# LayerNorm after two expert layers: from stages of their own into the last steps of the expert stages

## The reference, cut to what matters

```
x   = _layernorm(ALPHA * x   + g1 * y_lat, ln_w[layer, 0], ln_b[layer, 0])
f_lat = _peer(x * (1.0 + sc2) + sh2, ...)
x   = _layernorm(ALPHA * x   + g2 * f_lat, ln_w[layer, 1], ln_b[layer, 1])     # the norm of this case
ctx = _layernorm(ALPHA * ctx + cg2 * f_ctx, ln_w[layer, 1], ln_b[layer, 1])    # the same, first layer only
hl = x * (1.0 + sc1) + sh1                                                     # start of the next layer
hc = ctx * (1.0 + csc1) + csh1
```

## Time and profile before

| | before |
|---|---|
| median of 3 runs | 3768.81 us (3768.76 to 3774.37) |
| the profiled execution's own time | 3774.25 us |
| its span | 3772.4 us |
| PE busy | 3024.5 us (80%) |
| DVE busy | 1991.3 us (53%) |
| ACT busy | 791.2 us (21%) |
| POOL busy | 879.9 us (23%) |
| DMA | 1026.04 MB, 272 GB/s over the span |
| first norm stage with the barriers around it (end of last `take` to first `c_q` matmul) | 1845.9 to 1901.1 us |
| second norm stage with the barriers around it (end of last `take` to first `b_rms1` instruction) | 2945.4 to 2971.5 us |

### The profile page before, as it was taken

One profiled execution on the slowest core, in us unless ns is written; L12 is line 12 of the kernel. 1 busy time (PEld: TensorE's weight loads), 2 busy tenths in 40 slices (PEclk: granted clock), 3 DMA queues, 4 the chain that ended last, 5 costly groups with the idle time before them and its releaser, 6 DMA issues. The chain is left out here.

```text
span 3772.4 us, 28092 instructions
## 1 busy us (share of the span) xinstructions
PE 3024.5 (80%) x8564; PEld 1486.2 (39%) x8564; DVE 1991.3 (53%) x5057; ACT 791.2 (21%) x2002; POOL 879.9 (23%) x772
## 2 busy tenths in 40 slices
PE   7987788888888888777488667878877597897898
PEld 3444443333333333322243334333332355453663
DVE  1135567777777777776610756767776323223100
ACT  0112312222222222222101312222222130122000
POOL 0000014444444444444100003444444000000000
PEclk9996899999999999999788689999999898898999
DMA  5143229999999999999612247999999343323333
GB/s 195 57 157 112 90 114 427 427 427 427 427 427 423 423 421 417 426 416 427 262 45 91 90 157 322 427 427 427 427 427 427 142 139 116 112 105 130 112 134 122
DMA packets 238156, 1026.04 MB, mean 272 GB/s; under 512 B 41399, under 2 KB 46007, under 8 KB 137639
## 3 DMA queue, kind: packets, MB, share of 16 engines
q0 software_dynamic: 110592, 805.36, 50.8%
q1 hardware_dynamic: 126984, 217.63, 16.5%
q10 hardware_dynamic: 432, 1.31, 0.1%
HBM read 1023.10 MB, written 1.13 MB: 272 GB/s over the span
## 5 line engine op out<-in xcount | busy, mean ns | idle before, releaser
L1528 PE MATMUL l_peer_experts_acc<-l_peer_experts_ring,l_peer_experts_diag 128*128 128x512 f32 x1840 | 860.9, 610 | 217.3 <-ACT l_peer_experts_diag L1567 216.8
L1688 DVE SCALAR_TENSOR_TENSOR l_peer_experts_ring<-l_peer_experts_ring,h_tiles 128x1024 f32<-128x1024 f32 x460 | 563.6, 1225 | 287.4 <-DMA l_peer_experts_ring<-in_expert_rows,l_peer_experts_picks 283.9
L1528 PE MATMUL l_peer_experts_acc<-weight_slots,l_peer_experts_diag 128*128 128x512 f32 x1232 | 581.2, 614 | 150.9 <-ACT l_peer_experts_diag L1567 150.6
L1470 POOL DMA_INDIRECT weight_slots<-in_expert_rows,l_peer_experts_picks x308 | 348.1, 1130 | 1431.1 <-DVE l_peer_experts_picks L1647 1009.0
L1470 POOL DMA_INDIRECT l_peer_experts_ring<-in_expert_rows,l_peer_experts_picks x460 | 531.7, 1156 | 611.5 <-PE l_peer_experts_acc L1528 538.1
L1528 PEld LDWEIGHTS l_peer_experts_acc<-l_peer_experts_ring,l_peer_experts_diag 128*128 128x128 f32 x1840 | 337.4, 192 | 710.9 <-issue 397.3
L1688 DVE SCALAR_TENSOR_TENSOR weight_slots<-weight_slots,h_tiles 128x1024 f32<-128x1024 f32 x308 | 377.4, 1225 | 190.8 <-DMA weight_slots<-in_expert_rows,l_peer_experts_picks 188.3
L1528 PEld LDWEIGHTS l_peer_experts_acc<-weight_slots,l_peer_experts_diag 128*128 128x128 f32 x1232 | 227.9, 194 | 481.7 <-issue 274.7
L1560 ACT ACTIVATE l_peer_experts_gel<-l_peer_experts_dots 128x2 f32<-128x2 f32 x384 | 78.2, 204 | 1207.6 <-DVE l_peer_experts_ring L1688 727.1
L1567 ACT ACTIVATE l_peer_experts_diag<-const_ident,l_peer_experts_wgt 128x128 f32<-128x128 f32 x768 | 266.4, 394 | 225.8 <-DVE l_peer_experts_wgt L1664 209.8
L1495 PE MATMUL l_peer_experts_queries<-h_t,l_query_weights 128*128 128x512 f32 (+3 forms) x576 | 182.0, 461 | 3.9 <-PEq L61 3.9
(11 more groups left out here) (464 smaller groups left out, 3367.1 us busy)
## 6 DMA issues: line engine op xcount, KB each, us to landing
weight_slots<-in_w_mod SPq DMA_DIRECT2D x24, 2048.0 KB, 7.8
weight_slots<-in_w_in SPq DMA_DIRECT2D x20, 2048.0 KB, 7.7
l_query_weights<-query_weights SPq DMA_DIRECT2D x16, 1024.0 KB, 9.0
weight_slots<-in_w_mlp_up SPq DMA_DIRECT2D x8, 2048.0 KB, 7.8
weight_slots<-in_w_mlp_down SPq DMA_DIRECT2D x8, 2048.0 KB, 7.7
weight_slots<-in_gla_w_in SPq DMA_DIRECT2D x6, 2048.0 KB, 8.4
weight_slots<-in_ab_w_in SPq DMA_DIRECT2D x5, 2048.0 KB, 8.8
l_ln_rows<-mod_rows SPq DMA_DIRECT2D x16, 512.0 KB, 9.5
```

Source lines behind the costliest of these rows:

```text
L1470: pool.indirect_dma_start(rows(b, k, None), None, uv, bass.IndirectOffsetOnAxis(ap=picks[:, b % 4, k:k + 1], axis=0)).then_inc(landing(b, ...
L1528: ins = nc.tensor.matmul(acc[:, b % 2, c * BANK:(c + 1) * BANK], diag[:, k % DIAGS, :], row[:, c * BANK:(c + 1) * BANK], start=(k == 0), s ...
L1688: nc.vector.scalar_tensor_tensor(row, row, 1.0, h[:, tile_of(b), :], ALU.mult, ALU.mult, accum_out=dots[:, b % 2, k:k + 1]).then_inc(dotte ...
```

## The change

The two norm stages are gone. Their work is inside `stage_peer`:

- **Rows.** `LastNorm` puts gates, weight and bias (4 rows in the first layer, 3 in the second) into `wq_slots`. SP issues these loads in the expert stage as soon as the last projection is done.
- **Norm.** `normalise(tile, part)` splits the norm of one tile into seven parts on DVE. Each stands behind the dot of one k. In the first layer tile 0 has its parts in step 30, tile 1 in steps 30 and 31, tile 2 in step 31. In the second layer tile 0 has them in step 15. The last tile's seven parts come after the loop, behind the last `take`. The square roots stand in ACT's queue at fixed pairs of the last two steps (`root_at`), that of the last tile after the loop.
- **Modulation.** The four broadcast rows of scales and shifts and the two DVE instructions per tile are replaced. The scales and shifts are loaded as columns (`mod_cols`, four DMAs of 1024 single floats, first in SP's queue in the first layer's expert stage). PE transposes blocks of the normalised `x` instead of `h`, into the PSUM of the projections; ACT writes each block of 128x128 to `h_t` with the column of scales as its scale and that of shifts as its bias: eight instructions per tile instead of two. Tiles 0 and 1 are transposed ahead of k = 2 and k = 6 of the last step and modulated behind pairs 3 and 6; tiles 2 and 3 after the loop.
- **Weights.** SP issues `weights.begin` as soon as the last product has been added, with no row loads ahead of it.

```
 @block.sync
+    for i, (scale, shift) in enumerate(norm.mods):
+        for j, row in enumerate((scale, shift)):
+            sp.dma_start(mod_cols[:, i, j, :], row.rearrange("(c p) -> p c", p=P), allow_slow_non_contiguous=True).then_inc(mods_loaded, 16)
     ...
+    sp.wait_ge(q_done, len(units))
+    norm.load(sp, wq_slots, rows_loaded)
+    sp.wait_ge(added, steps * TOPK // 2)
+    weights.begin(sp)

+    norm_at, root_at = {}, {}
+    for tile in range(group - 1):
+        first, at, pair = {3: (steps - 2, (0, 1, 2, 3, 6, 7, 8), 1), 2: (steps - 2, (9, 10, 11, 12, 15, 16, 17), 6),
+                           1: (steps - 1, (5, 6, 7, 8, 11, 12, 13), 4)}[group - 1 - tile]
+        root_at[first, pair] = tile
+        for part, k in enumerate(at):
+            norm_at[first + k // TOPK, k % TOPK] = (tile, part)

 @block.tensor
+    def turn(tile):
+        pe.wait_ge(made, tile + 1)
+        if tile:
+            pe.wait_ge(emptied, 2 * tile)
+        else:
+            pe.wait_ge(q_taken, len(units))
+        for half in range(2):
+            for c in range(4):
+                at = (4 * half + c) * P
+                last = nc.tensor.transpose(q_ps[:, half, c * P:(c + 1) * P], x[:, tile, at:at + P], ident)
+            last.then_inc(turned, 1)
     ...
+        if norm.mods and b == steps - 1 and k in (2, 6):
+            turn(k // 4)
     ...
+    if norm.mods:
+        for tile in range(2, group):
+            turn(tile)

 @block.scalar
+    def modulate(tile):
+        i = norm.mod_of[tile]
+        for half in range(2):
+            act.wait_ge(turned, 2 * tile + half + 1)
+            for c in range(4):
+                k = 4 * half + c
+                last = nc.scalar.activation(h_t[:, k, tile * P:(tile + 1) * P], q_ps[:, half, c * P:(c + 1) * P], ACT.Identity,
+                                            scale=mod_cols[:, i, 0, k:k + 1], bias=mod_cols[:, i, 1, k:k + 1])
+            last.then_inc(emptied, 1)
     ...
+        if (b, j) in root_at:
+            root(root_at[b, j])
+        if norm.mods and b == steps - 1 and j in (3, 6):
+            if j == 3:
+                act.wait_ge(mods_loaded, 32 * len(norm.mods))
+            modulate(j // 3 - 1)
+    root(group - 1)
+    if norm.mods:
+        for tile in range(2, group):
+            modulate(tile)

 @block.vector
+    def normalise(tile, part):     # part 0: gate * y   1: ALPHA * x + y   2: bn_stats x2   3: bn_aggr, + epsilon
+        ...                        # part 4: wait for the root, reciprocal, (x - mean) * rstd   5: * weight   6: + bias
     ...
+        if (b, k) in norm_at:
+            normalise(*norm_at[b, k])
         if k % 2:
             weigh(b, k // 2)
     take(steps - 1)
+    for part in range(7):
+        normalise(group - 1, part)
```

More of the change, by code:

```diff
@@ L637, in load @@
             eng.dma_start(dst, src).then_inc(mod_sem if mod_sem is not None and i >= self.norm_rows else sem, 16)
[L640 to L737, removed]
@@ L1372, with __init__, row, load @@
 UV_SLOTS = 10
-def stage_peer(nc, name, h, h_t, group, n_groups, wq, wq_slots, wq_loaded, wq_before, k_t, uv, iota, ident, layer, y, slots, landed, before0):
+class LastNorm:
+    def __init__(self, gates, ln, mods=(), mod_of=()):
+        self.sources = [row for _, row in gates] + list(ln)
+        self.gate_of = {tile: i for i, (tiles, _) in enumerate(gates) for tile in tiles}
+        self.mods, self.mod_of = mods, mod_of
+        self.n_rows = len(self.sources)
+    def row(self, buffer, i):
+        return buffer.rearrange("p s k n -> p (s k n)")[:, i * D:(i + 1) * D]
+    def load(self, eng, buffer, sem):
+        for i, source in enumerate(self.sources):
+            eng.dma_start(self.row(buffer, i), source.partition_broadcast(P)).then_inc(sem, 16)
+    def gate(self, buffer, tile):
+        return self.row(buffer, self.gate_of[tile])
+    def weight(self, buffer):
+        return self.row(buffer, self.n_rows - 2)
+    def bias(self, buffer):
+        return self.row(buffer, self.n_rows - 1)
+def stage_peer(nc, name, h, h_t, group, n_groups, wq, wq_slots, wq_loaded, wq_before, k_t, uv, iota, ident, layer, y, slots, landed, before0, x, norm, weights):
     DIAGS = TOPK // 2
@@ L1434, in stage_peer @@
         share = scratch[:, 448:480].rearrange("p (i k) -> p i k", k=TOPK)
+        stats = st.sb("ln_stats", [P, 2, 6])
+        agg = st.sb("ln_agg", [P, group, 2])
+        std = st.sb("ln_std", [P, group])
+        rstd = st.sb("ln_rstd", [P, group])
+        mod_cols = st.sb("ln_mod_cols", [P, max(1, len(norm.mods)), 2, KC])
+        rows_loaded, mods_loaded, var_ready, std_ready, made, turned, emptied = (
+            st.sem(f"ln_{n}") for n in ("rows_loaded", "mods_loaded", "var_ready", "std_ready", "made", "turned", "emptied"))
         names = ("dotted added scored scores_read chosen gelu_done soft_in soft_out w_ready diag_ready sum_taken "
@@ L2513, in buffers, with peer @@
     return lambda name, shape, dt=F32: ctx.enter_context(nc.sbuf_tensor(name, shape, dt))
[L2516 removed]
+def peer(nc, weights, name, layer, group, n_groups, consts, a, wq, keys_t, h, h_t, y, landed, before0, x, norm):
     stage_peer(nc, f"{name}_experts", h, h_t, group, n_groups, *wq, keys_t[:, :, :], a["expert_rows"], consts["iota"][:, :], consts["ident"][:, :], layer, y,
[L2519 removed]
+               weights.slots[:, :, :, :], landed, before0, x, norm, weights)
 def mixer_ab(nc, weights, consts, a, cat, h_t, y, mod0, mod1):
@@ L2730, in build @@
                 peer(nc, weights, "l0_peer", 0, *L0_GROUP, consts, a, (wq, wq_slots[:, :, :, :], wq_loaded, 0), keys_t, h[:, :, :], h_t[:, :, :],
[L2731 to L2735, removed]
+                     y[:, :, :], landed, 0, x, LastNorm([((0, 1), row(0, True, 5)), ((2, 3), row(0, False, 5))], ln(0, 1),
+                                                        [(row(1, context, 1), row(1, context, 0)) for context in (True, False)], (0, 0, 1, 1)))
             mixer_c(nc, weights, consts, a, h, h_t, y, mod_args[1])
@@ L2747, in build @@
                 peer(nc, weights, "l1_peer", 1, LT, 1, consts, a, (wq, wq_slots[:, :, :, :], wq_loaded, 16 * HEADS * L0_GROUP[1] // 2), keys_t,
[L2748 to L2751, removed]
+                     h[:, 0:LT, :], h_t[:, :, :], y[:, 0:LT, :], landed, HEADS * TT * TOPK, x[:, 2:4, :], LastNorm([((0, 1), row(1, False, 5))], ln(1, 1)))
         second_block(nc, weights, consts, a, x[:, 2:4, :], x[:, 0:2, :], out)
```

29 lines of the change are left out of this document (added).

## The result

| | before | changed |
|---|---|---|
| median | 3771.59 us (3768.76 to 3774.49, 4 runs) | 3726.95 us (3718.44 to 3732.09, 4 runs) |
| ratio | | 0.9877, 95% interval 0.9866 to 0.9888 |
| span of the profiled execution | 3772.4 us | 3726.1 us |
| from first gather to last dot, first / second layer | 1292.1 / 651.4 us | 1298.2 / 655.3 us |
| from last dot to last sum, first / second layer | 6.24 / 6.24 us | 6.76 / 6.24 us |

The kernel is 1.2% faster: 44.6 us between the medians, 46.3 us between the two spans, 47.6 predicted.

What follows compares the result with a forecast made beforehand. DMA bytes bound the expert stages, and the tails between them are plain chains. Gains of 41.1 and 16.3 less 9.8 us for rows give 47.6, from 3768.81 to 3721.2 us; 3711 to 3735 for 8 in 10.

Steps and rivals of the forecast that it cites:

- Tail of the first layer: From the first layer's last sum to `c_q`: 14.1 us against 55.2, a gain of 41.1 us.
- Tail of the second layer: From the second layer's last sum to `b_rms1`: 9.8 us against 26.1, a gain of 16.3 us.
- The collision of the weights with `b_rms1`'s rows: Second layer's tail: early weight tiles may delay `b_rms1`'s row loads, up to 1.5 us possible, taken as 0.
- The rows: Seven 512 KB loads moved into the DMA-bound expert stages: 1.4 us each, 9.8 us lost, bounds 8.6 to 17.5.
- The columns: Four column loads at the start of the first expert stage, while the DMA is idle: cost 0.
- the slower rival: First expert stage: column loads share DMA engines with the gathers; at 20 us each the time is 3801 us; chance 0.02.
- The last steps: End of the expert loops: DVE, PE and ACT cover the parts, cost 0, bound 2 us a layer; falling behind, chance 0.12.
- the lag of 0.7 us: DVE in the last step: 0.7 us behind the pace at k = 13, gone at k = 14.
- PE: two turns of 2.0 us ... made up in two pairs, the second by k = 10: PE in the last step: two turns of 2.0 us beside 3.7 of 4.9 us per pair, made up, cost 0.
- the gap from the last landing to the last product: End of the last step: over 6.2 us here would show the prediction wrong.
- ScalarE's switches: ACT's roots in the loop: 2.8 us each without drain; draining rival 3725 to 3728 us, chance 0.09 together with dear rows.
- PE's clock: PE at `c_q` after the tail: no change in granted clock, with 2.6 us to either side.

Runs made afterwards that it cites:

- e2: The changed kernel with the seven broadcast rows loaded a second time behind the first, in the DMA-bound part; 3735.29 us.
- e4: The changed kernel with the second layer's three broadcast rows loaded at the start of its expert stage, into idle tiles of h and y; 3722.34 us, ratio 0.9872.
- e7: The changed kernel with sixteen instead of four column loads ahead of the query weights in SP's queue; 3724.35 us (1 run).
- e3: The changed kernel with tile 1 transposed ahead of k = 10 of the last step instead of k = 6; 3725.05 us.

## Why the prediction was right

The mechanism holds: tails that are a plain chain, a DMA-bound loop in which only the rows' bytes cost, and norm work that the loop covers. Term by term the sum is within 1.4 us: 40.7 gained for 41.1, 16.0 for 16.3, 9.9 lost for 9.8, and 0.5 lost at the last product for 0. That the profiled execution as a whole came within 1.2 us is in part luck: the stretches outside moved by 5.2 us down and 4.0 up and happened to cancel.

- **Tail of the first layer:** 14.1 us predicted, 1868.87 - 1854.35 = 14.5 measured. The eight ACTIVATEs took 2.9 us for 3.0, one of them 462 ns for 457. The missing 0.4 us is the end of the stage, 2.34 us from the last ACTIVATE to `c_q` for 1.8: I had 0.03 us per semaphore from one pair of stages, and the runs give 0.055 to 0.07.
- **Tail of the second layer:** 9.8 predicted, 10.1 measured, with 0.3 from the same cause. The collision of the weights with `b_rms1`'s rows didn't show: DVE waits 4.18 us for the rows, 4.90 before.
- **The rows:** 9.8 us predicted, 9.9 in the profile, 9.3 as the mean over the experiments (5.4 + 3.9). e2 shows the cost directly, and e4 that it goes where the DMA is idle. The 1.4 us a row was the least certain price; the 1.2 to 1.35 measured lie between it and the lower bound of 1.23. The last product came 8.5 us later than before: 6.0 by the rows, inside the "5 to 7", 1.9 by the later first gather and 0.5 by the stall below.
- **The columns** cost nothing that shows (e7); the slower rival falls with them. **The weights** for `c_q` were there in time: it started as soon as the barrier let it.
- **The last steps:** DVE waited for a landing again at k = 15 as predicted, but not at k = 14, where it ran straight on from k = 13. The dot of k = 13 starts at 1841.48, 4.88 us before the one of k = 15 that waits for its landing. That is two rows of the pace (4.92), so the lag of 0.7 us that I had counted isn't there. The step that failed is "PE: two turns of 2.0 us ... made up in two pairs, the second by k = 10". I had costed the turns as work and overlooked the wait in front of the second one: `emptied`, which ACT gives only after it has modulated tile 0, behind the diagonals of k = 6 and 7. It cost some 3 of the 4.1 us that PE stands there, and 0.5 us of the span (0.4 to 1.4 over the profiles), inside the 2 us a layer that I had as a bound, but for another reason. One sign that I had named for being wrong did appear: the gap from the last landing to the last product was to stay within 6.2 us and is 1853.09 - 1846.36 = 6.7. The kernel before has 6.20, so the sign left no room, and it caught this step. The turns themselves were too dear in my sum: 1.04 and 1.06 us for 2.0. ACT's covers were thinner than I had them: behind the three roots it still idled 0.5 to 0.9 us as predicted, but the gelu behind each modulation followed without a pause, where I had 0.7 us to spare.
- **ScalarE's switches:** no drain shows. Around the first root in the loop:

```profile
1779.01 0.69 ACT L1555 ACTIVATE l_peer_experts_diag<-const_ident,l_peer_experts_wgt 128x128 f32<-128x128 f32 x2 [0.52 <-DVE l_peer_experts_wgt L1662]
1779.72 1.28 ACT L1524 ACT_TABLE_LOAD   x1
1781.02 0.20 ACT L1524 ACTIVATE l_peer_experts_ln_std<-l_peer_experts_ln_agg 128x1 f32<-128x1 f32 x1
1781.24 1.28 ACT L1548 ACT_TABLE_LOAD   x1
1783.02 0.20 ACT L1548 ACTIVATE l_peer_experts_gel<-l_peer_experts_dots 128x2 f32<-128x2 f32 x1 [0.50 <-DVE l_peer_experts_ring L1716]
```

  Root and both loads take 2.8 us, and ACT then has 0.5 us to wait for its next dot. The Trainium skill's 2.66 us a switch ("ScalarE: Activation LUTs", section "What ACT_TABLE_LOAD costs") would have made this 5.5, an estimate; the measurement decides against it here.
- **PE's clock** before and after a tail: `c_q` took 15.45 us instead of 16.55, but 17.04 when the changed kernel was profiled again, and 15.5 to 17.1 in the experiments. So "no change" holds, and the 1.1 us aren't a gain of the change. The clock over the mixer, where the profiles differ by 10 us, was not in the prediction; only the 5.6 us between the runs before stood for it.

## What to carry to other kernels

Work moved from a stage of its own into a DMA-bound loop cost nothing here as long as its engine caught up before the last product, but each byte moved there with it cost its full share; so look for a time when the DMA is idle, and for idle memory, before placing a load. Cost a moved instruction with the waits in front of it, not only its duration: the one real stall came from a shared PSUM buffer whose release stood in another engine's queue. When a change is worth a few us in a long kernel, compare the stretches of the profiles that it touches, since the untouched ones alone scattered by more.

## What the runs showed of the hardware beyond that

- The end of a stage took longer the more semaphores GpSimd clears: 1.34 us with 8, 2.06 with 21, 2.98 with 34 (second layer), so 0.055 to 0.07 us each. The change itself paid for this, twice.
- Broadcast rows of 512 KB that landed some 1.5 us apart when loaded alone cost 1.2 to 1.35 us each among the gathers (e2).
- After PE had idled 4.11 us its next eight matmuls of the experts' product ran at a mean granted clock of 0.68, 5.30 us instead of 3.70. Where the idle time was 1.1 to 1.3 us (e3) they took 3.70.
- In the same code, the mean granted PE clock of the mixer stretch was 0.82 to 0.85 over the profiles, with 386.6 to 376.9 us.
